# Decode attention, differential keys: turned in 32x32 blocks by the vector engine instead of by matrix transposes; four key pages ahead of the values instead of two

## The reference, cut to what matters

```python
# cache_diff_kv (.., N_PHYS, PAGE_SIZE=128, 2, DIFF_HEADS=8, DIFF_DV=128): rows [k1|k2 normed, v]
s_diff = cache_diff_kv[l][page_table].reshape(DB, past_len, 2, DIFF_HEADS, DIFF_DV)
s1 = jnp.einsum('bqhd,bkhd->bhqk', q1b, k1) * scale + bias      # k1 = first 64 of the 128, k2 = the rest
s2 = jnp.einsum('bqhd,bkhd->bhqk', q2b, k2) * scale + bias
a = masked_softmax(s1, mask) - lam * masked_softmax(s2, mask)
return jnp.einsum('bhqk,bkhd->bqhd', a, v)
```

## Time and profile before

| | us |
|---|---|
| median of 3 runs | 1718.29 (1717.81 to 1719.01) |
| profiled execution, its time | 1718.2 |
| profiled execution, its span | 1716.4 |
| TensorE matmul busy | 1603.7 (93%) |
| VectorE busy | 808.1 (47%) |
| ScalarE busy | 570.8 (33%) |
| GpSimd busy | 180.4 (11%) |

### The profile page before, as it was taken

One profiled execution on the slowest core, in us unless ns is written; L12 is line 12 of the kernel. 1 busy time (PEld: TensorE's weight loads), 2 busy tenths in 40 slices (PEclk: granted clock), 3 DMA queues, 4 the chain that ended last, 5 costly groups with the idle time before them and its releaser, 6 DMA issues. The chain is left out here.

```text
span 1716.4 us, 31637 instructions
## 1 busy us (share of the span) xinstructions
PE 1603.7 (93%) x12648; PEld 1329.8 (77%) x12648; DVE 808.1 (47%) x1841; ACT 570.8 (33%) x1185; POOL 180.4 (11%) x269
## 2 busy tenths in 40 slices
PE   6999999998999988799899899889799999999997
PEld 4878888876888875577777776666488999999996
DVE  4576632215443428776766545445355442234322
ACT  4233220223323226656555233233233331133210
POOL 2001000000630000073212000000000000000000
PEclk9999999999999998999999899999899999999998
DMA  8855443434631316344121499998542334334321
GB/s 272 308 172 170 165 139 141 144 84 102 183 105 28 105 38 183 84 173 138 44 77 38 169 386 369 370 347 294 220 143 89 123 103 117 122 99 135 84 73 53
DMA packets 184201, 265.67 MB, mean 155 GB/s; under 512 B 35661, under 2 KB 115917, under 8 KB 183958
## 3 DMA queue, kind: packets, MB, share of 16 engines
q1 hardware_dynamic: 174934, 227.57, 40.4%
q0 software_dynamic: 6016, 25.34, 4.9%
q10 hardware_dynamic: 3136, 11.22, 1.7%
HBM read 241.01 MB, written 42.60 MB: 165 GB/s over the span
## 5 line engine op out<-in xcount | busy, mean ns | idle before, releaser
L648 PE MATMUL pj_ps<-all_hi,pj_xh 128*128 128x512 f32 x480 | 191.7, 399 | 1.5 <-DVE all_lo L536 1.5
L649 PE MATMUL pj_ps<-all_lo,pj_xh 128*128 128x512 f32 x480 | 190.0, 396 | 0.0
L650 PE MATMUL pj_ps<-all_hi,pj_xl 128*128 128x512 f32 x480 | 189.9, 396 | 0.0
L1427 ACT ACTIVATE pa_sc<-pa_sc,pa_nmax 128x32 f32<-128x32 f32 (+4 forms) x256 | 126.0, 493 | 115.7 <-DVE pa_nmax L1476 115.5
L2685 PE MATMUL fi_ps<-fi_fl,fi_wh 128*128 128x272 f32 x512 | 149.2, 291 | 0.0
L2686 PE MATMUL fi_ps<-fi_fh,fi_wl 128*128 128x272 f32 x512 | 148.4, 290 | 0.0
L2684 PE MATMUL fi_ps<-fi_fh,fi_wh 128*128 128x272 f32 x512 | 148.3, 290 | 0.0
L2686 PE MATMUL fi_ps<-fi_th,fi_wl 128*128 128x272 f32 x512 | 148.3, 290 | 0.0
L2684 PE MATMUL fi_ps<-fi_th,fi_wh 128*128 128x272 f32 x512 | 147.6, 288 | 0.7 <-DVE fi_tl L2486 0.7
L2685 PE MATMUL fi_ps<-fi_tl,fi_wh 128*128 128x272 f32 x512 | 147.2, 287 | 0.0
L2069 ACT ACTIVATE de_slot<-de_ps_t 128x512 f32<-128x512 f32 (+5 forms) x124 | 62.8, 513 | 175.3 <-PE de_ps_t L1903 85.6
(11 more groups left out here) (328 smaller groups left out, 3175.3 us busy)
## 6 DMA issues: line engine op xcount, KB each, us to landing
de_dv<-in_cache_diff SPq DMA_DIRECT2D x64, 512.0 KB, 9.7
all_big<-in_w_in SPq DMA_DIRECT2D x14, 2048.0 KB, 10.1
de_dk<-in_cache_diff SPq DMA_DIRECT2D x48, 512.0 KB, 8.7
all_big<-in_cache_nsa SPq DMA_DIRECT2D x64, 256.0 KB, 6.4
all_big<-in_w_up SPq DMA_DIRECT2D x16, 1024.0 KB, 5.6
all_big<-in_w_down SPq DMA_DIRECT2D x16, 1024.0 KB, 5.5
all_win<-in_cache_win SPq DMA_DIRECT2D x32, 256.0 KB, 7.9
all_dk<-in_cache_diff SPq DMA_DIRECT2D x16, 512.0 KB, 8.7
```

What stands on the lines that cost most here:

```text
L648: pe.matmul(ps[:, t, :], xh[:, k, xk], hi(k), start=k == 0, stop=False)
L649: pe.matmul(ps[:, t, :], xh[:, k, xk], lo(k), start=False, stop=False)
L650: ins = pe.matmul(ps[:, t, :], xl[:, k, xk], hi(k), start=False, stop=k == KT - 1)
L1427: nc.scalar.activation(tile, tile, ACT.Exp, scale=-1.0, bias=nmax[:, x.n % 6, a:a + 1], accum_out=x.sums[a]).then_inc(probs, 1)
```

## The change

The differential keys are no longer turned by TensorE. A key page of a pair is loaded by four DMAs instead of two. Each takes one sequence (b) and one half of the heads (c, 512 numbers of a row) and writes to 32 partitions, 64b + 32c to 64b + 32c + 31: partition j of them gets the tokens j, 32 + j, 64 + j and 96 + j, 2 KB of each. VectorE then turns the whole tile of 128x2048 in place, block by block of 32x32 (`turn_keys`), so that the partitions hold b, c and 32 of the 128 numbers of a head. TensorE multiplies straight from this tile: 16 matmuls a page as before, each over both sequences and both halves at once. The "dif" and "dif_n" steps have no `turn` and no copy any more (`on_pe`); the other steps' copies are dealt out anew between ScalarE and VectorE. The queries and the new keys get tiles of 32-row blocks (`qd_rows`, `dk_n`), filled by small DMAs and turned by VectorE too. A key buffer is free when the page has been multiplied. Rows of the score tile have a new order, so the bias is loaded by 16 DMAs of 8 rows. `KEYS_FIRST` goes from 2 to 4, and keys 6 and 7 are loaded ahead of the next pair's sparse pages.

```diff
 KEY_PAGES, KEYS_AHEAD = 4, 1
-N_CONSTS = 14
+N_CONSTS = 22
...
-        for j in range(2):
-            heads = slice(HEADS + 4 * j, HEADS + 4 * j + 4)
+        for h in range(4):
             for m in range(2):
-                at = rows.start + 32 * j + 16 * m
-                sp.dma_start(a.b_dif[at:at + 16, :], d["decb"][heads, :, 0:NCOL].rearrange("h t k -> (h t) k")
-                             ).then_inc(g.consts_in, 16)
+                at = 32 * h + 16 * b + 8 * m
+                sp.dma_start(a.b_dif[at:at + 8, :], d["decb"][HEADS + h:HEADS + DHEADS:4, :, 0:NCOL]).then_inc(g.consts_in, 16)
...
 def key_load(sp, d, g, pages, i, k):
+
     n = (N_PAGES * i + k) % KEY_PAGES
+    keys = d["cache_diff"].rearrange("n (q j) e -> n j q e", j=32)
     for b in range(2):
-        sp.dma_start(g.ahead.dk[n][:, b, :], d["cache_diff"][bass.ds(pages[b][k], 1), :, 0:1024]
-                     .rearrange("n p e -> (n p) e")).then_inc(g.dk_in[n], 16)
+        for c in range(2):
+            at = 64 * b + 32 * c
+            sp.dma_start(key_tile(g.ahead.dk[n])[at:at + 32, :, :], keys[bass.ds(pages[b][k], 1), :, :, CW * c:CW * (c + 1)]
+                         .rearrange("n j q e -> (n j) q e")).then_inc(g.dk_in[n], 16)
...
-KEYS_FIRST = 2
+KEYS_FIRST = 4
...
-        owner = ["act" if g % 2 == 0 else "dve" for g in range(N)]
-        for g in CHOOSE_AT:
-            for n, eng in ((1, "act"), (2, "act"), (3, "act"), (5, "dve"), (6, "dve"), (9, "act"), (10, "act")):
-                owner[g + n] = eng
+        on_pe = [kind not in ("dif", "dif_n") for _, kind, _, _ in STEPS]
+        turns = [sum(on_pe[:g + 1]) for g in range(N)]
+        owner = [("act" if turns[g] % 2 or kind in ("p_sel", "p_few", "p_win") else "dve") if on_pe[g] else None
+                 for g, (_, kind, _, _) in enumerate(STEPS)]
         level = [owner[:g + 1].count(owner[g]) for g in range(N)]
+        ring = [(n - 1) % 4 for n in turns]
+
+        def keys_free(n):
+
+            i, k = divmod(n, N_PAGES)
+            return (scores_mm, NG * i + GROUP_OF["dif", k] + 1) if k % 4 == 3 else (keys_read, 6 * i + k - k // 4 + 1)
+
+        KEYS_AT = {max(AT[i, "dif", k, 0] - 4, AT[i, "dif_n", 0, 0] if k < KEY_PAGES else 0): [] for i in pairs for k in range(N_PAGES)}
...
-                sp.dma_start(dk_n, split(d["diff_s"][new, 0:1024])).then_inc(new_in, 16)
+
+            def load_diff_rows(i):
+
+                for b in range(2):
+                    at = 2 * DEC_T * i + DEC_T * b
+                    for c in range(2):
+                        cols = slice(CW * c, CW * (c + 1))
+                        rows = 64 * b + 32 * c
+                        sp.dma_start(dk_n[rows:rows + DEC_T, :], d["diff_s"][at:at + DEC_T, cols]).then_inc(dk_n_in, 16)
+                        for m in range(2):
+                            row = rows + 16 * b + 8 * m + 4 * c
+                            part_of = lambda ap: ap.rearrange("t (h m e) -> t h m e", h=4, m=2)[:, :, m, :]
+                            sp.dma_start(part_of(qd_rows[row:row + DEC_T, :]),
+                                         part_of(d["qd"][SEQ + at:SEQ + at + DEC_T, cols])).then_inc(dq_in, 16)
...
-                    sp.wait_ge(turned, AT[n // N_PAGES, "dif", n % N_PAGES, 3] + 1)
+                    sp.wait_ge(*keys_free(n))
                 key_load(sp, d, shared, pages, i, k)
 
             load_new(0)
             for k in range(KEYS_AHEAD, KEY_PAGES):
                 load_k(shared.pages[0], 0, k)
+            sp.wait_ge(rows_zeroed, 2)
+            load_diff_rows(0)
             load_new_v(0)
...
                 load_dv_new(i)
+                load_k(pages, i, 6)
+                load_k(pages, i, 7)
                 sp.wait_ge(nsa_mm, i + 1)
                 sel_load(sp, d, shared, following, range(0, 3))
                 load_new(i + 1)
-                load_k(pages, i, 6)
+                load_diff_rows(i + 1)
                 sel_load(sp, d, shared, following, range(3, 6))
                 load_new_v(i + 1)
-                load_k(pages, i, 7)
...
-                elif kind == "dif":
-                    n = N_PAGES * i + k
-                    if m == 0:
-                        pe.wait_ge(dk_in[n % KEY_PAGES], 32 * (n // KEY_PAGES) + 32)
-                    for b in range(2):
-                        for x in range(2):
-                            c, h = 2 * b + x, m + 4 * x
-                            ins = pe.transpose(bank[:, P * c:P * (c + 1)], dk[n % KEY_PAGES][:, b, P * h:P * (h + 1)], ident[:])
...
+                    elif m == 0:
+                        if k in (0, 4) and NG * i + GROUP_OF[kind, k] > 1:
+                            pe.wait_ge(scored, NG * i + GROUP_OF[kind, k] - 1)
+                        pe.wait_ge(keys_turned, N_PAGES * i + k + 1)
+                    for h in range(4):
+                        ins = pe.matmul(bank[32 * h:32 * h + 32, at:at + n], qdb[:, i % 2, 4 * h + m, :], keys[:, 4 * h + m, :, :],
+                                        start=m == 0, stop=m == 3)
...
             def lay_diff_queries(i):
 
-                for m in range(2):
-                    half = slice(DD * m, DD * (m + 1))
...
+                dve.wait_ge(dq_in, 128 * i + 128)
+                nc.vector.transpose(qdb[:, i % 2, :, :].rearrange("p f c -> p (f c)"), qd_rows[:]).then_inc(qdb_ready, 1)
+
+            def turn_keys(i, k):
+                n = N_PAGES * i + k
+                dve.wait_ge(dk_in[n % KEY_PAGES], 64 * (n // KEY_PAGES) + 64)
+                tile = dk[n % KEY_PAGES][:].rearrange("p b e -> p (b e)")
+                nc.vector.transpose(tile, tile).then_inc(keys_turned, 1)
...
+                if g < N and STEPS[g][1:] == ("dif_n", 0, 0):
+                    dve.wait_ge(dk_n_in, 64 * STEPS[g][0] + 64)
+                    nc.vector.transpose(dk_n[:], dk_n[:]).then_inc(dk_n_turned, 1)
+                for i, k in KEYS_AT.get(g, ()):
+                    turn_keys(i, k)
```

More of the change, by code:

```diff
@@ L1724, in decode_attention @@
         NSA_AT = {AT[i, "p_win", 0, 0] + 4: i for i in pairs}
-        Q_STEP = {AT[i - 1, "p_win", 0, 0] + 14: i for i in range(1, PAIRS)}
+        Q_STEP = {AT[i - 1, "p_win", 0, 0] + 6: i for i in range(1, PAIRS)}
         QB_AT = after(Q_STEP, 1)
@@ L1812, in _ @@
                 sp.wait_ge(q_turned, i + 1)
-                sp.wait_ge(turned, AT[i, "cmp", 0, 0] + 1)
+                sp.wait_ge(turned, turns[AT[i, "cmp", 0, 0]])
                 pair_rows(sp, d, shared, i + 1)
@@ L1889, in turn @@
                             c = 2 * b + x
-                            h = m + 4 * x if kind == "dif_n" else x
-                            ins = pe.transpose(bank[:, DEC_T * c:DEC_T * (c + 1)], src[:, b, P * h:P * (h + 1)], ident[one, one])
+                            ins = pe.transpose(bank[:, DEC_T * c:DEC_T * (c + 1)], src[:, b, P * x:P * (x + 1)], ident[FEW_ROWS, FEW_ROWS])
                 elif kind == "cmp":
@@ L1928, in multiply @@
                 i, kind, k, m = STEPS[g]
-                tile = slot[:, g % 4, :]
-                pe.wait_ge(copied[owner[g]], level[g])
+                tile = slot[:, ring[g], :]
+                if on_pe[g]:
+                    pe.wait_ge(copied[owner[g]], level[g])
                 ins = None
-                if kind in ("sel", "win", "sel_n", "win_n", "cmp", "dif", "dif_n"):
+                if kind in ("dif", "dif_n"):
                     bank, at = score_place(i, kind, k)
[L1934 to L1938, removed]
-                        pe.wait_ge(qdb_ready, i + 1)
-                        if i:
-                            stand()
-                            pe.wait_ge(few_read, 2 * i)
-                    elif kind == "dif_n" and m == 0:
+                    if kind == "dif_n":
+                        n, keys = DEC_T, dk_n[:].rearrange("p (f q j) -> p f q j", f=16, q=1)[:, :, :, 0:DEC_T]
+                    else:
+                        n, keys = P, key_tile(dk[(N_PAGES * i + k) % KEY_PAGES]).rearrange("p q (f j) -> p f q j", f=16)
+                    if kind == "dif_n" and m == 0:
                         stand()
@@ L1959, in multiply @@
                                 c = P * x + CMPS * b
-                            ins = pe.matmul(bank[rows, at:at + n], lhs, tile[:, c:c + n], start=m == 0,
-                                            stop=m == 3 or kind not in ("dif", "dif_n"))
-                    if kind == "win_n" or (kind == "dif_n" and m == 3):
+                            ins = pe.matmul(bank[rows, at:at + n], qb[:, x, b, :], tile[:, c:c + n], start=True, stop=True)
+                    if kind == "win_n":
                         ins.then_inc(few_mm, 1)
@@ L2020, in turn_queries @@
                     half, at = slice(DK * (g % 2), DK * (g % 2 + 1)), Q_AT + 32 * (g // 2) + 8 * h
-                    pe.matmul(ps_n[half, at:at + 8], qn[:, DK * x:DK * (x + 1)], ident[0:2 * DEC_T, 0:2 * DEC_T],
-                              start=True, stop=True)
-                one = slice(32, 32 + 2 * DEC_T)
```

(31 more changed lines are left out.)

58 lines of the change are left out of this document (40 added, 18 removed).

## The result

| | before | after |
|---|---|---|
| median (4 runs each, same chip) | 1718.05 us | 1821.47 us (1815.84 to 1836.59) |
| profiled execution, its span | 1716.4 us | 1823.2 us |
| first load of new rows in the decode stage | 965.6 | 980.8 |
| first load of the closing stage | 1240.7 | 1350.7 |
| decode stage, between these two | 275.1 us | 369.9 us |

The ratio is 1.062, 95% interval 1.055 to 1.068. The change makes the kernel 103 us slower in the medians. Between the two profiled spans lie 106.8 us: 94.8 in the decode stage, 15.2 ahead of it, and -3.2 behind it.

A forecast was written before the change was run, and what follows sets the result against it. The full DMA queue bounds the decode stage: 228 + 94 = 322 us of full queue, plus start, last page and tail, ends the stage at 1320 for 1240.7, 79 us later: 1797 us. Range 1775 to 1820; 8 in 10, 1764 to 1824.

The forecast's parts named there:

- The rate of the key loads: Decode stage: loads to 32 partitions move 184 GB/s, 5.70 us a page for 2.68, costing 94 us more DMA time.
- rival A: Key loads: few partitions don't matter, halves overlap, 332 GB/s upwards decides; 1703 us, chance 0.08.
- rival B: Key loads: partial overlap of halves, 4.19 us a page (250 GB/s), 1750 us; chance 0.10.
- Alternating halves gives nothing: Key loads: all 16 engines are in the same half together, so changing halves after every second load gains nothing.
- The start: First pair: VectorE waits for query rows behind key pages 1 to 3; key page 4 late, queue gap about 5 us.
- The end of the queue: End of decode loads: last load lands at 1297 us, last key page 8 us earlier at 1289.
- The last page: After the last key lands: one turn of 2.44 us and 16 matmuls of 0.65 us, until 1292.
- The tail behind it: From the last key matmuls to the closing stage's first load: same work as before, 27.7 us.
- TensorE's saving is worth nothing: Decode stage: at least 78 of TensorE's 231 us go, but beside a longer queue, counted at nothing.
- VectorE: Decode stage: work grows from 119 to about 153 us, turns 2.44 us each; only the last turn is paid.
- Rival D: Decode stage: VectorE or small loads become their own wait, 1805 to 1815 us; chance 0.77 together with the forecast.
- The order of pages and loads: Decode stage, KEYS_FIRST and load order: queue stays full, costs nothing; 0 to 5 us a pair if wrong.

The follow-up runs named there:

- e3: Kernel before, each key load split into partitions 0 to 63 and 64 to 127, pieces still 4 KB: ratio 1.052, stage 360.9 us.
- e5: Kernel after, key loads reordered so the lower and upper 64 partitions alternate after every load: ratio 1.049 to the kernel before, stage 355.9 us.
- e6: Kernel after, key loads to the upper 64 partitions issued on GpSimd's queue, the lower on SP's: ratio 1.047 to the kernel before, stage 353.1 us.
- e9: Kernel after, key loads to 128 partitions in 2 KB pieces, small row loads issued earlier on SP: ratio 1.006 to the kernel before, stage 284.1 us.
- e11: Kernel after, key loads to 128 partitions in 2 KB pieces, old order of pages and loads: ratio 1.023 to the kernel before, stage 313.2 us.
- e2: Kernel before, key loads replaced by the kernel after's four loads to 32 partitions, 2 KB pieces: ratio 1.054, stage 361.4 us.
- e4: Kernel before, each key load split into two 256 KB loads to all 128 partitions, 2 KB pieces: ratio 1.003, stage 276.8 us.

## Why the prediction was right, and where it was off

It said slower, 1797 us, by the DMA queue; it came out 24 us above that, inside the range. By its steps:

- **The rate of the key loads** was the step that decided, and it held in kind: the queue is full, keys flow at little more than half rate, and rival A (332 GB/s and up) is out. 184 GB/s was too low for the keys themselves: their windows show 206 to 221, or 4.81 us a page at 218, and 31 x (4.81 - 2.68) = 66 us. That lies between the forecast (5.70 us a page) and rival B (4.19). But the sum of 94 us of full queue held, with 90 measured. The difference was paid by the neighbours: in the trace's packet times, value packets of 4 KB took 198 ns on average for 174 (median 165 for 160, the slowest tenth over 309 for 171), which is 8760 x 24 / 16 / 1.06 = 12 us. The packets of the sparse pages and windows have the keys' size in the kernel after, but not in e3, where they took 113 ns for 91: 10304 x 22 / 16 / 1.06 = 13 us. 66 + 12 + 13 = 91 us. e3's window at 1200 us has keys and values mixed at 228 GB/s. The packet times are measured; that they rise because engines that have drifted apart carry values while others still carry keys is an inference. So rows of short bursts overstated the cost of the keys and left out that of the neighbours, and the two errors cancelled by luck.
- **Alternating halves gives nothing** was a premise of the 184, and it held only in part: 252 GB/s in e5 where the half changes after every load, 299 in e6 with two queues.
- **The start** was predicted as a gap of 5 us with key 4 issued 37 us after the first key load. It was 41.5, and the queue stood at share 0.14 for 10 us. The wait for the query rows was foreseen (17.5 us, until 1001.8). What stood behind it in VectorE's order was not counted: copies, score reads and the choice of pages until 1018, then the turn of the first key page.
- **The end of the queue.** From first key load to last load the forecast had 330 us, the trace has about 333: the DMA share falls from 1.04 at 1312 us to 0.39 at 1314 and 0.19 at 1315. The last key, though, landed at 1314.9, together with the last values and not 8 us ahead of them, although it stood three value pages ahead in the queue. Predicted 322 us after the first key load, measured 333: 11 of the missing 16 us.
- **The last page** was taken at 2.44 + 0.65 us. The turn took 2.3. The timeline of the end shows the rest:

```profile
1314.89 2.31 DVE L2203 STREAM_TRANSPOSE de_dk<-de_dk 128x2048 f32<-128x2048 f32 x1 [2.56 <-DMA de_dk<-in_cache_diff]
...
1317.26 1.08 PE L1976 MATMUL de_ps_s<-de_dk,de_qdb 128*32 128x128 f32 x16 [2.94 <-DVE de_dk L2203]
...
1318.27 3.78 PE L1935 MATMUL de_ps_t<-de_cm,de_s_sel 128*128 128x128 f32 x16
...
1321.98 0.94 PE L1976 MATMUL de_ps_s<-de_dk,de_qdb 128*32 128x128 f32 x16
```

  The trace has 32 matmul records a page, not 16, and TensorE turns two steps ahead: 16 transposes of the value steps stand between the halves of the last page, at the clock's lower level (0.50). 5.7 us for 0.65: the other 5 us. The tail behind it took 27.8 us, predicted 27.7.
- **TensorE's saving is worth nothing**: confirmed. It is busy for 190 of 345 us and waits 113 us for turned keys (90.4 in the row, 22.5 for `all_dk`).
- **VectorE** was predicted at 153 us and has 145; turns take 2.30 us, 2.44 predicted. No run shows it as a bound of its own: in e9, with full-rate loads and early rows, it is busy for 151 of 285 us. Rival D's small loads are real as a wait of VectorE, but beside a full queue they cost no more than the start's gap.
- **The order of pages and loads** at nothing: e11 puts it at a gain of 10 us where the rate is full.
- **Ahead of the stage**, 15 us weren't in the sum, and they carry the profiled spans from +91 to +107. 4 us are there before the first constant is loaded, in stages that the change doesn't touch. Of the other 11, 8 come after the last prompt heads' store (939.2 to 965.6 before, 946.1 to 980.8 after), where the granted clock is 0.50 to 0.53 for the kernel after and was 0.92 from 950 to 966 us for the kernel before:

```profile
957.00:965.00 8.00, 7.85 (x39) 7.79 (x40) 2.17 (x7) 1.14 (x4) 0.91 (x2) 0.53 0.00 0
965.00:981.00 16.00, 10.20 (x47) 9.56 (x45) 4.12 (x9) 0.92 (x2) 1.81 (x4) 0.50 0.06 17
```

  From the load of the constants to the decode stage the kernels with before's code took 266 to 270 us in 4 profiles, those with after's 266 to 281 in 10. The 8 us behind the last store show in only 2 of these 10 (34.7 us in the profile of the result, 34.8 in e11); the others have 26.4 to 27.6, like the kernel before with 26.4. Whether the change has a part in it (its 8 further bias loads run there) stays open: no run took them out.

In all: +79 us predicted for the stage, +95 measured, 11 of the difference from where the last key lands and 5 from the last page.

## What to carry to other kernels

Before an edit that saves an engine's work by reshaping a load, look at the load first: one whose destination lies in partitions 0 to 63 or 64 to 127 ran here at 200 to 252 GB/s for 389, with pieces of 2 and of 4 KB, and the loads around it slowed down too. Only with both halves in flight on two queues did it come to 299. With the DMA queue full, that outweighed TensorE's saving. Where the queue is not the bound, small loads that an in-order engine waits for belong ahead of the big ones in the queue's order; moving them to another queue was no substitute.

## What the runs showed of the hardware beyond the forecast

- Loads to 32 and to 64 partitions of one half cost the same: stages of 361.4 and 360.9 us for 276.8 at 128 partitions (e2, e3, e4).
- Key loads to one half moved 214 to 228 GB/s when the half changed after every second load (kernel after, e2), 230 to 252 when it changed after every load (e3, e5), and 239 to 299 from two queues, one for each half, while both held keys (e6); 2 KB pieces to all 128 partitions moved 389 (e4).
- Value packets next to half-width loads took 198 ns on average for 174, though their own shape was unchanged.
- VectorE's turn of 128x2048 fp32 in 32x32 blocks, in place, took 2.30 us (24 of 2301 ns, 8 of 2290 ns), 1.9 times that of 1024 columns.
